# A two-block transformer kernel: the first scores of its dilated attention wait for the group root, its first fill is evicted ahead of the exponentials, and the merge's RWKV parts are formed beside the last values

## The reference, cut to what matters

```
n = rmsnorm(h, norm_mix_g); proj = n @ w_in
y_rwkv = rwkv7_mix(...)          # 16 heads; ends with a group norm over each head's 64 channels:
    yn = (y - mean) * rsqrt(var + GN_EPS) * gn_w + gn_b
    return (yn + bonus) * g
y_attn = dilated_mixture(q, k, v)    # 3 groups of 4 heads, windows 128/512/2048, dilations 1/4/16,
    # banded softmax with ALiBi bias, the groups mixed by the softmax of their logsumexps
merged = sigmoid(gate_r) * (y_rwkv @ p_rwkv) + sigmoid(gate_a) * (y_attn @ p_attn)
h = h + merged @ w_out
h = h + memory_cross_attention(rmsnorm(h), rmsnorm(mem), ...)   # mem: 256 tokens
```

## Time and profile before

| | |
|---|---|
| three runs | 2968.95, 2955.92, 2965.5 us (median 2965.5) |
| profiled execution | 2954.55 us, of which the span 2952.6 |
| busy: PE, PEld, DVE, ACT, POOL | 2752.6, 2007.0, 1709.6, 645.8, 188.5 us |
| granted TensorE clock, mean | 0.968 of full speed |
| chain that ended last | PE 86%, DVE 8%, issue 3%, ACT 1% |
| the stretch of the change | about 2042 to 2217 us from the span's start |

### The profile page before, as it was taken

The page is one execution under the profiler, slowest core; times in us unless marked ns, Lnnn a source line. Parts: engine busy times, 40 slices in busy tenths (PEclk is TensorE's granted clock), DMA queues, the critical chain, the costliest instruction groups (busy, mean ns, idle before and its releaser), DMA issues.

```text
span 2952.6 us, 42986 instructions
## 1 busy us (share of the span) xinstructions
PE 2752.6 (93%) x17241; PEld 2007.0 (68%) x17241; DVE 1709.6 (58%) x2286; ACT 645.8 (22%) x1089; POOL 188.5 (6%) x203
## 2 busy tenths in 40 slices
PE   4799787999999999999989999998989999999998
PEld 3455443788887878888655555565557788788887
DVE  7677775655547665554456555663345575655554
ACT  3133412211101021110132223321341121211002
POOL 2000121000010010000030000010000010100001
PEclk8999898999999999999999999998999999999999
DMA  7466401333332323333211111111203333223332
GB/s 237 127 209 207 125 11 43 92 96 88 98 99 81 97 78 99 92 92 97 74 34 32 42 46 34 37 37 47 59 24 92 96 90 112 84 87 100 93 98 72
DMA packets 393989, 255.46 MB, mean 87 GB/s; under 512 B 19879, under 2 KB 376832, under 8 KB 393728
## 3 DMA queue, kind: packets, MB, share of 16 engines
q1 hardware_dynamic: 390256, 243.63, 28.0%
q0 software_dynamic: 2320, 5.11, 0.6%
q10 hardware_dynamic: 1280, 4.78, 0.4%
HBM read 250.60 MB, written 2.10 MB: 86 GB/s over the span
## 4 chain that ended last, share of the span: by engine, by line
PE 86%; DVE 8%; issue 3%; ACT 1%; DVEq 0%; DMA 0%; POOL 0%; ACTq 0%; SPq 0%; POOLq 0%
PE PS L827 14%; PE PS L826 14%; PE PS L828 14%; PE PS L1532 4%; PE PS L1507 3%; PE PS L841 3%; PE PS L842 3%; PE PS L843 3%; PE PS L813 3%; PE PS L1265 3%; PE PS L1598 1%; PE PS L1513 1%; PE PS L1624 1%; PE PS L1622 1%; PE PS L1718 1%
## 5 line engine op out<-in xcount | busy, mean ns | idle before, releaser
L852 DVE CAST WH<-W 128x1024 fp32r<-128x1024 f32 x304 | 213.3, 702 | 417.7 <-PE PS L828 371.9
L827 PE MATMUL PS<-XNL,WH 128*128 128x512 f32 x960 | 382.0, 398 | 0.0
L854 DVE TENSOR_TENSOR WL<-W,WH 128x1024 fp32r<-128x1024 f32 x304 | 374.5, 1232 | 10.4
L826 PE MATMUL PS<-HH,WH 128*128 128x512 f32 x672 | 262.3, 390 | 0.1
L827 PE MATMUL PS<-HL,WH 128*128 128x512 f32 x672 | 261.7, 389 | 0.0
L828 PE MATMUL PS<-HH,WL 128*128 128x512 f32 x672 | 261.7, 389 | 0.0
L827 PEld LDWEIGHTS PS<-XNL,WH 128*128 128x128 f32 x960 | 181.0, 189 | 41.5 <-issue 0.5
L828 PE MATMUL PS<-XNH,WL 128*128 128x512 f32 x512 | 201.7, 394 | 0.0
L826 PE MATMUL PS<-XNH,WH 128*128 128x512 f32 x512 | 201.2, 393 | 0.0
L826 PE MATMUL PS<-XN2H,WH 128*128 128x512 f32 x448 | 178.7, 399 | 10.7 <-issue 6.8
L828 PE MATMUL PS<-XN2H,WL 128*128 128x512 f32 x448 | 177.7, 397 | 0.0
(11 more groups left out here) (499 smaller groups left out, 4727.3 us busy)
## 6 DMA issues: line engine op xcount, KB each, us to landing
ARENA<-in_ada_w SPq DMA_DIRECT2D x80, 512.0 KB, 4.9
W<-in_ffn_w SPq DMA_DIRECT2D x64, 512.0 KB, 3.8
W<-in_w_in SPq DMA_DIRECT2D x51, 512.0 KB, 4.1
W<-in_ffn_w_gate SPq DMA_DIRECT2D x44, 512.0 KB, 3.8
W<-in_ffn_w_up SPq DMA_DIRECT2D x44, 512.0 KB, 3.8
W<-in_ffn_w_down SPq DMA_DIRECT2D x32, 512.0 KB, 3.7
W<-in_sc_w_in SPq DMA_DIRECT2D x24, 512.0 KB, 3.7
W<-in_ada_w SPq DMA_DIRECT2D x16, 512.0 KB, 4.7
```

Of the source, the lines that this page charges most:

```text
L826: nc.tensor.matmul(dst, WH[:, h, c], hi(k), start=(start and k == 0), stop=False)
L827: nc.tensor.matmul(dst, WH[:, h, c], lo(k), start=False, stop=False)
L852: nc.vector.tensor_copy(WH[:, h, :], W[:, s, 0:D]).then_inc(parted, 1)
L854: nc.vector.tensor_tensor(WL[:, h, :], W[:, s, 0:D], WH[:, h, :], ALU.subtract).then_inc(freed[s], 1)
```

## The change

On TensorE, the first scores wait for `groot` and for `yc` instead of `groot` and `out`. The first three k steps of fill unit 1 stand ahead of scores 2 instead of behind. The transposes of the memory go to banks 4, 6, 7, 3 and no longer wait for the copy o1; merge unit 3, which writes bank 3, waits for the memory copy e3. On ScalarE, the copy of unit 0 stands ahead of the first exponential; the high parts of YR stand ahead of o1, those of YA behind it, then the two memory copies, then the high parts of XN. On VectorE, a wait for `out` stands ahead of the first bias addition; the low parts of YR follow the last probabilities; then, after a wait for the last values, the split of unit 0, the low parts of YA, the split of unit 1, the two memory copies, the low parts of XN.

```diff
--- before.py
+++ after.py
@@ -554,7 +554,7 @@
         dil_turns = lambda n: " ".join(f"t{n}{g}" for g in range(NG))
         dl_pe = prog("dl_pe", "s0 s1 " + dil_steps(lambda n: (f"s{n + 2} " if n + 2 < DIL_STEPS else "") + (f"pv{n // 4 - 1} " if n and n % 4 == 0 else "")
                                                    + dil_turns(n)) + " pv3")
-        dl_act = prog("dl_act", "exp0 u0 " + dil_steps(lambda n: (f"exp{n + 1} " if n + 1 < DIL_STEPS else "") + ("o0 " if n == 8 else "") + dil_turns(n)
+        dl_act = prog("dl_act", "u0 exp0 " + dil_steps(lambda n: (f"exp{n + 1} " if n + 1 < DIL_STEPS else "") + ("o0 " if n == 8 else "") + dil_turns(n)
                                                        + (f" u{DIL_FILL[n]}" if n in DIL_FILL else "")) + " o1")
         dl_dve = prog("dl_dve", "b0 max0 " + dil_steps(lambda n: (f"b{n + 1} max{n + 1} " if n + 1 < DIL_STEPS else "") + f"inv{n} p{n}"))
         mem_pe, mem_act, mem_dve = prog("mem_pe", "t0 t1 t2 t3"), prog("mem_act", "e0 e2"), prog("mem_dve", "e1 e3")
@@ -619,6 +619,7 @@
         assert KD * T + 2 * T + 5 * NG * T + NG * NT * T + DIL_UNITS * T + NC * D <= NARENA - DIL_UNITS * T
         DIL = (DIL0, DIL1)
         DL_TURN = (3, 4, 6)
+        MEM_BANK = (4, 6, 7, 3)
         w_tail = lambda b, j: W[:, 2 * b + j, KD * P:SLOT].rearrange("p (k n) -> p k n", n=P)
 
 
@@ -1705,7 +1706,7 @@
             pair_pass(RW_PAIRS - 1, 0, rz_pe, rz_act, rz_dve, rz_pool, False)
 
             pe.wait_ge(rz_act.sem, rz_act.done("groot"))
-            pe.wait_ge(rz_dve.sem, rz_dve.done("out"))
+            pe.wait_ge(rz_dve.sem, rz_dve.done("yc"))
             def scores(n):
 
                 half, e, qt = n // 8, n // 4 % 2, n % 4
@@ -1757,11 +1758,13 @@
             fill(0, range(KD))
             scores(1)
             for n in range(DIL_STEPS):
+                if n == 0:
+                    fill(DIL_FILL[n], range(0, 3))
                 if n + 2 < DIL_STEPS:
                     scores(n + 2)
                 if n and n % 4 == 0:
                     values(n // 4 - 1)
-                if n in DIL_FILL:
+                if n and n in DIL_FILL:
                     fill(DIL_FILL[n], range(0, 3))
                 for g in range(NG):
                     turn(n, g)
@@ -1771,11 +1774,10 @@
 
 
             pe.wait_ge(mem_in, 16)
-            pe.wait_ge(dl_act.sem, dl_act.done("o1"))
             for m in range(4):
                 for n in range(4):
                     c0 = (2 * m + n // 2) * P
-                    mm = nc.tensor.transpose(bank[m][:, n * P:(n + 1) * P], MEMTOK[:, n % 2, c0:c0 + P], IDENT)
+                    mm = nc.tensor.transpose(bank[MEM_BANK[m]][:, n * P:(n + 1) * P], MEMTOK[:, n % 2, c0:c0 + P], IDENT)
                 mm.then_inc(mem_pe.sem, mem_pe.step(f"t{m}"))
 
             xn2_hi = lambda k: XN2H[:, k, :]
@@ -1785,6 +1787,8 @@
             with pe.Fori(0, KD) as i:
                 for u, (hi, lo, kts, parts) in enumerate(operands):
                     pe.wait_ge(mg_dve.sem, mg_dve.before("ra"[u % 2], i))
+                    if u == 3:
+                        pe.wait_ge(mem_dve.sem, mem_dve.done("e3"))
                     split_product(pe, "merge", u, i, bank[u], hi, lo, kts,
                                   ready={k: (mp_dve.sem, mp_dve.done(step)) for k, step in parts.items()}).then_inc(multiplied, 1)
             norm_pe(pe, norm_mem2, MN, TC, 7)
@@ -2267,8 +2271,8 @@
                 act.wait_ge(dl_pe.sem, dl_pe.done(f"pv{2 * half + 1}"))
                 nc.scalar.activation(YA[:, half, :], bank[5], ACT.Copy).then_inc(dl_act.sem, dl_act.step(f"o{half}"))
 
+            filled(0)
             exps(0)
-            filled(0)
             for n in range(DIL_STEPS):
                 if n + 1 < DIL_STEPS:
                     exps(n + 1)
@@ -2283,17 +2287,22 @@
                                                      bank[DL_TURN[g]][:, 0:(qt + 1) * P].rearrange("p (c t) -> p c t", t=P), ACT.Copy).then_inc(dl_act.sem, dl_act.step(f"t{n}{g}"))
                 if n in DIL_FILL:
                     filled(DIL_FILL[n])
+            def high_parts(own):
+
+                for step, hi, x in merge_parts[own]:
+                    nc.scalar.activation(hi, x, ACT.Copy).then_inc(mp_act.sem, mp_act.step(step))
+
+            act.wait_ge(rz_dve.sem, rz_dve.done("out"))
+            high_parts(slice(0, KD))
             head_pair(1)
-
+            act.wait_ge(dl_act.sem, dl_act.done("o1"))
+            high_parts(slice(KD, KD + 2))
             for m in (0, 2):
                 act.wait_ge(mem_pe.sem, mem_pe.done(f"t{m}"))
-                nc.scalar.activation(MEM[:, 2 * m:2 * m + 2, :], bank[m].rearrange("p (k t) -> p k t", k=2), ACT.Copy).then_inc(mem_act.sem, mem_act.step(f"e{m}"))
-
+                nc.scalar.activation(MEM[:, 2 * m:2 * m + 2, :], bank[MEM_BANK[m]].rearrange("p (k t) -> p k t", k=2), ACT.Copy).then_inc(mem_act.sem, mem_act.step(f"e{m}"))
+            high_parts(slice(KD + 2, None))
             act.wait_ge(mem_act.sem, mem_act.done("e2"))
             act.wait_ge(mem_dve.sem, mem_dve.done("e3"))
-
-            for step, hi, x in merge_parts:
-                nc.scalar.activation(hi, x, ACT.Copy).then_inc(mp_act.sem, mp_act.step(step))
             norm_act_squares(act, norm_mem2, MEM, MN)
 
             with act.Fori(0, KD) as i:
@@ -2950,6 +2959,7 @@
                 dve.wait_ge(dl_dve.sem, dl_dve.done(f"b{n}"))
                 nc.vector.tensor_reduce(NEGMAX2[:, at:at + 1], own(n), AXXY, ALU.max, negate=True).then_inc(dl_dve.sem, dl_dve.step(f"max{n}"))
 
+            dve.wait_ge(rz_dve.sem, rz_dve.done("out"))
             biased(0)
             row_max(0)
             for n in range(DIL_STEPS):
@@ -2962,16 +2972,21 @@
                 dve.wait_ge(dl_dve.sem, dl_dve.done(f"inv{n}"))
                 ts(own(n), own(n), total, None, ALU.mult).then_inc(dl_dve.sem, dl_dve.step(f"p{n}"))
 
+            def low_parts(own):
+
+                for (step, hi, x), lo in zip(merge_parts[own], merge_lows[own]):
+                    dve.wait_ge(mp_act.sem, mp_act.done(step))
+                    tt(lo, x, hi, ALU.subtract).then_inc(mp_dve.sem, mp_dve.step(step))
+
+            low_parts(slice(0, KD))
+            dve.wait_ge(dl_pe.sem, dl_pe.done("pv3"))
+            split_unit(dve, "merge", 0, 0)
+            low_parts(slice(KD, KD + 2))
+            split_unit(dve, "merge", 1, 0)
             for m in (1, 3):
                 dve.wait_ge(mem_pe.sem, mem_pe.done(f"t{m}"))
-                nc.vector.tensor_copy(MEM[:, 2 * m:2 * m + 2, :], bank[m].rearrange("p (k t) -> p k t", k=2)).then_inc(mem_dve.sem, mem_dve.step(f"e{m}"))
-            dve.wait_ge(mem_pe.sem, mem_pe.done("t3"))
-            for u in range(2):
-                split_unit(dve, "merge", u, 0)
-
-            for (step, hi, x), lo in zip(merge_parts, merge_lows):
-                dve.wait_ge(mp_act.sem, mp_act.done(step))
-                tt(lo, x, hi, ALU.subtract).then_inc(mp_dve.sem, mp_dve.step(step))
+                nc.vector.tensor_copy(MEM[:, 2 * m:2 * m + 2, :], bank[MEM_BANK[m]].rearrange("p (k t) -> p k t", k=2)).then_inc(mem_dve.sem, mem_dve.step(f"e{m}"))
+            low_parts(slice(KD + 2, None))
 
             with dve.Fori(0, KD) as i:
                 for u in range(4):
```

## The result

| | before | after |
|---|---|---|
| median of 8 runs | 2963.93 us (2954.4 to 2968.95) | 2945.51 us (2940.76 to 2950.18) |
| ratio, 95% interval | | 0.9947 (0.9935 to 0.996) |
| profiled execution, span | 2954.55, 2952.6 us | 2943.49, 2941.6 us |

By the ratio the change is 0.53% faster, between 0.4 and 0.65%: some 15.7 us of the runs (11.9 to 19.3). The spans of the two profiled executions differ by 11.0 us. They don't start level: the end of the group root, with the same code ahead of it, comes at 2043.04 in the one and 2045.01 in the other, and anywhere from 2042.2 to 2050.0 in the thirteen profiles of this study. From that root to the end it is 909.56 us before and 896.59 after, **13.0 us less**, and this is how all profiles are compared here.

The account below looks back on a forecast made before the run. TensorE, busy 93% of the span, was taken as the bound. Terms 5.7 + 1.0 + 0.5 + 6.4 - 1.7 gave 11.9 us less; off the 2965.5 median, 2953.6, named as 2953, range 2941 to 2962.

Parts of the forecast that it names:

- the bound of 0.5%: Whole kernel: 14.8 us, about what a measurement can tell from no change; chances 0.70 same, 0.26 faster, 0.04 slower.
- Scores wait for the root alone: Start seam: first scores start 0.15 us behind the root on ScalarE, 5.7 us earlier.
- Clock at the start: Behind the first scores: the rise from half clock comes a little sooner, 0.5 us gained, ends 0 and 2.0.
- the third rival: From first scores through the fill: clock stays low, kernel slower, 2968 us; chance 0.04.
- Fill 1 ahead of scores 2: Start seam: three products of fill 1 replace TensorE's wait before scores 2; 1.0 us gained, ends 0 and 1.3.
- Between the seams: Sixteen steps from start to merge: the start's gain passes whole, 5.7 + 1.0 + 0.5 = 7.2 us.
- Rival (b): In the steps: TensorE comes early, then waits for VectorE or a weight tile; gain only 4.7 us, 2961; chance 0.10.
- Merge unit 2: Merge seam: VectorE's shorter chain behind the last values lets this unit start 6.4 us earlier, ends 5.5 and 6.7.
- Clock at the end: Merge units 2 and 3: half clock for 3.5 us behind a 4.7 us wait, minus 1.7 us, ends 0 and 2.2.
- the sign of being right: Before merge unit 2: a TensorE wait of 4 to 5 us on L854, with a low clock behind it.
- Rival (a): Both seams: early clock rise (+1.5) and no fall over the gap (+1.7), 15.1 us, 2950; gain over 14.8 us: 0.26.
- Rival (c): First scores through fill: clock stays low, decisive past 24 us beyond 2056 (12 gained); 2968 us, chance 0.04.

Follow-up runs that it names:

- early splits: The whole change, with VectorE also splitting merge units 0 and 1's weights before YR's low parts, after the second values; 2944.0 us, ratio to before 0.9938.
- part 1: Kernel before, with only the first scores waiting for yc and the root, and VectorE for out before the first bias addition; ratio 0.9976.
- part 2: Kernel before, with only unit 0 copied ahead of exponential 0 and three k steps of fill 1 ahead of scores 2; ratio 0.9985.
- part 3: Kernel before, with only the change's merge reordering and new banks for the memory's transposes; ratio 0.998.

## Why the prediction was right

The median lies in the range, 7.5 us under the 2953 named, the interval lies across the bound of 0.5%, and the mechanism at both seams is the one forecast. What the clock did in three places, at the first scores, behind scores 2 and in the cross-attention, was not. Term by term, against the profiled execution that the sum was made for:

- *Scores wait for the root alone*: 5.7 forecast, 5.83 - 0.05 = 5.78 measured.
- *Clock at the start*: +0.5 forecast. Scores 0 to scores 1 took 11.21 us instead of 11.36: +0.15. But **this is the step that failed**, because one profile stood for the kernel. In six of the seven executions with the old wait the scores-to-scores stretch was 10.0 to 10.2 us, and 11.4 only in the one I had; with the new wait it is 11.2 to 11.3 in all six. Against a typical execution the term is about -1.2, a loss, in the direction that the text named only for the third rival.
- *Fill 1 ahead of scores 2*: 1.0 forecast; 7.42 us from scores 1 to the first transposes became 6.40, 1.02. It held for that profile too. Against a typical execution, 9.07 became 6.40: 2.7. The missing 1.6 is the clock that falls behind the wait, which the forecast had not priced. That the two misses cancel is luck: 5.8 - 1.2 + 2.7 = 7.3, and 24.9 - 17.65 is 7.25, where the forecast had 7.2.
- *Between the seams*: of 6.95 us at the first transposes 6.81 arrive at the last values. Rival (b) falls.
- *Merge unit 2*: 6.4 forecast, 26.66 - 19.71 = 6.95. VectorE's chain behind the last values took 2204.78 - 2191.84 = 12.9 us, not 13.5: successive steps overlap, two copies in 1.28, a split in 1.87 from start to start. The upper end, 6.7, came from this and was too low.
- *Clock at the end*: -1.7 forecast, 11.16 - 12.74 = -1.6 measured from unit 2 to the second round, in every profile with the 3.9 us wait. The wait was forecast at 4.7, with 4 to 5 us as the sign of being right, and took 3.85: shorter, since unit 2 came earlier and units 0 and 1 took 7.1, not 6.7 us.

With the 0.14 us lost between the seams these sum to 12.2; root to end has 13.0 (13.4 against the three profiles). What is left lies in the cross-attention, where no code changed: from the first product of the memory's keys to that of the output 92.0 us before and in early splits, 91.0 after. All of it is at its first scores, behind a wait of 2.54 us that both kernels have. Before, with the stretch behind the wait:

```profile
2445.46 4.34 PE L1874 MATMUL PS<-ARENA 128*128 128x256 f32 x12 [2.54 <-DVE ARENA L3024]
```

```profile
2445.50:2447.50 2.00, 2.00 (x5) 1.64 (x6) 0.00 (x0) 0.00 (x0) 0.00 (x0) 0.50 0.61 185
```

After:

```profile
2435.28 1.97 PE L1878 MATMUL PS<-ARENA 128*128 128x256 f32 x8 [2.54 <-DVE ARENA L3039]
```

```profile
2435.30:2437.30 2.00, 1.95 (x8) 1.39 (x8) 0.44 (x2) 0.42 (x2) 0.00 (x0) 1.00 0.60 177
```

The clock is at 0.50 behind the wait before and at 1.00 after, and from these scores to the first product of the memory's values it is 3.99 us before and 3.00 after. It is 3.93 to 4.16 in the eight profiles of before, part 1, part 2 and early splits, and 2.99 to 3.00 in the five others, which all have part 3 and not the early splits. So this 1.0 us comes with part 3 (it is why that part is worth 6.3 us from root to end and 5.4 at round 2), no term of the forecast had it, and early splits lose it again. Why the clock falls in the one group and not in the other stays open. 12.2 and 1.0 are 13.2; 0.2 is lost again behind.

The runs' 15.7 us have 13 inside their interval. Rival (a) named a gain over 14.8 us, and the runs' 15.7 lie above that; but its mechanism didn't come: the rise was late and the clock fell over the gap. Rival (c): the rise was later than usual, by a price of 1.2 us, nowhere near its 12.

The exponential's table load was as in the earlier trace rows: it ends at 2058.33 and the exponential starts at 2058.35, so the trace does not agree with the drain that the Trainium skill (ScalarE: Activation LUTs, "What ACT_TABLE_LOAD costs") adds to a switch.

## What to carry to other kernels

When a wait is removed, ask who sets the next one, and compute the new idle time in front of it, for the clock behind it counts where TensorE sets the pace. One profile is one draw of the clock: where a term hangs on when the clock rises or falls, look at the kernel before several times, and compare from a landmark behind the untouched part. A stretch that no edit touches can change its clock too, so compare it as well before its gain is put down to the edit. An engine that waits for the last values may be waiting for much less: name the last reader of the memory, not of the stage.

## What the hardware showed that was not expected

A wait of 1.05 us between the narrow scores (64 rows, 256 and 384 columns) was followed by 0.50 in three executions of five, the three in which the clock had risen early in fill 0; a wait of 1.88 us before unit 2 in early splits, among dense products, left it at 1.00. The wait of 2.54 us before the first scores of the cross-attention, with the same code around it, was followed by 0.50 in eight profiles and by 1.00 in five, and every kernel profiled more than once stayed on its side. And how long the clock stayed low behind the first scores fell into two narrow groups, not a spread: the 16 matmuls of fill 0 took 8.5 to 8.7 us or 9.7 to 9.9, and the six profiles with the new wait all had the second. What picks the group stays open.
